# Second gather buffer, three 2 MB weight loads held until its rows have landed, and 30 fill transposes in the router of a decoder-layer kernel

## The reference

```python
m, new_a, new_b, v = token_mixer(x, ...)          # projections, convolutions, norms
h = layer_norm(ALPHA * x + m, ln1_g, ln1_b)
# moe_ffn(h): router, then experts
logits = h @ router_w + router_b
probs = softmax(logits)                            # best group of 4 by its top-2 sum, its top 2 experts, weights
for e in range(16):
    u = silu(h @ w_gate[e]) * (h @ w_up[e])        # 1024 x 512 each
    out = out + gates[:, e:e+1] * (u @ w_down[e])  # 512 x 1024
y = layer_norm(ALPHA * h + out, ln2_g, ln2_b)
```

## Time and profile before

| what | value |
|---|---|
| median of 3 runs | 1049.32 us |
| profiled execution, its own time | 1048.14 us |
| its span | 1046.4 us |
| TensorE busy | 995.1 us (95%), mean granted clock 0.978 |
| VectorE busy | 792.4 us (76%) |
| ScalarE busy | 473.1 us (45%) |
| GpSimd busy | 372.4 us (36%) |
| moved by DMA | 190.52 MB, 182 GB/s over the span |
| busy share of the DMA engines, in tenths, 40 slices | 7433232323232221333235534548899999999574 |
| granted TensorE clock, in tenths, 40 slices | 9999999999999999999999999997899999999995 |

### The profile page before, as it was taken

The page is one execution under the profiler, slowest core; times in us unless marked ns, Lnnn a source line. Parts: engine busy times, 40 slices in busy tenths (PEclk is TensorE's granted clock), DMA queues, the critical chain, the costliest instruction groups (busy, mean ns, idle before and its releaser), DMA issues.

```text
span 1046.4 us, 19478 instructions
## 1 busy us (share of the span) xinstructions
PE 995.1 (95%) x7212; PEld 901.5 (86%) x7212; DVE 792.4 (76%) x965; ACT 473.1 (45%) x665; POOL 372.4 (36%) x275
## 2 busy tenths in 40 slices
PE   7999999999999999999999999995999999999980
PEld 7999999999999998999999999974677777777760
DVE  2698889888999995744434598147789898999986
ACT  4232222323232244334442323424678787878763
POOL 2444434444544770445454544410110000000362
PEclk9999999999999999999999999997899999999995
DMA  7433232323232221333235534548899999999574
GB/s 220 122 93 95 85 100 81 100 80 100 81 101 81 80 82 49 100 110 89 81 99 170 172 90 144 208 163 317 300 368 391 375 391 379 383 388 393 203 253 165
DMA packets 163400, 190.52 MB, mean 182 GB/s; under 512 B 6675, under 2 KB 114195, under 8 KB 163340
## 3 DMA queue, kind: packets, MB, share of 16 engines
q1 hardware_dynamic: 156619, 177.65, 49.8%
q0 software_dynamic: 3008, 10.55, 3.2%
q10 hardware_dynamic: 3729, 1.75, 0.7%
HBM read 179.16 MB, written 11.76 MB: 182 GB/s over the span
## 4 chain that ended last, share of the span: by engine, by line
PE 57%; issue 25%; POOL 12%; DVE 3%; DMA 2%; ACT 1%; POOLq 0%; DVEq 0%
PE pr L986 27%; PE pr L1172 16%; POOL w_lo L562 12%; PE work L1172 8%; PE work L1148 1%; DMA hs<-h_rows,ids 1%; PE work L1069 1%; PE pr L1198 1%; DVE w_gate_lo L1625 1%; PE pr L1088 1%; PE work L1191 1%; DMA y_b<-y_rows,slot_b 1%; DVE y_a L1793 0%; PE work L1096 0%; DVE y_b L1789 0%
## 5 line engine op out<-in xcount | busy, mean ns | idle before, releaser
L562 POOL TENSOR_TENSOR w_lo<-raw,w_hi 128x512 fp32r<-128x512 f32 x208 | 298.0, 1453 | 334.5 <-ACT w_hi L680 334.5
L986 PE MATMUL pr<-x_hi,w_hi 128*128 128x260 f32 x1264 | 255.0, 283 | 0.2 <-POOL w_lo L562 0.2
L986 PE MATMUL pr<-x_hi,w_lo 128*128 128x260 f32 x1264 | 254.7, 283 | 0.0
L986 PE MATMUL pr<-x_lo,w_hi 128*128 128x260 f32 x1264 | 254.3, 283 | 0.0
L684 ACT ACTIVATE ev<-pr 128x520 f32<-128x520 f32 x96 | 58.1, 605 | 375.1 <-PE pr L986 375.1
L986 PEld LDWEIGHTS pr<-x_hi,w_hi 128*128 128x128 f32 x1264 | 195.0, 189 | 0.5 <-POOL w_lo L562 0.4
L986 PEld LDWEIGHTS pr<-x_hi,w_lo 128*128 128x128 f32 x1264 | 195.0, 188 | 0.0
L986 PEld LDWEIGHTS pr<-x_lo,w_hi 128*128 128x128 f32 x1264 | 194.4, 188 | 0.0
L1355 DVE SCALAR_TENSOR_TENSOR work<-b_pad,par,work 128x512 f32<-128x512 f32 x224 | 148.2, 743 | 0.0
L680 ACT ACTIVATE w_hi<-raw 128x512 fp32r<-128x512 f32 x208 | 118.9, 623 | 4.9 <-DMA raw<-in_w_in_dram 2.6
L599 POOL DMA_INDIRECT hs<-h_rows,ids x16 | 20.2, 1260 | 256.4 <-DVE ids L1619 246.6
(11 more groups left out here) (337 smaller groups left out, 1704.5 us busy)
## 6 DMA issues: line engine op xcount, KB each, us to landing
raw<-in_w_in_dram SPq DMA_DIRECT2D x80, 512.0 KB, 3.7
w_gate<-in_expert_w_gate_dram SPq DMA_DIRECT2D x16, 2048.0 KB, 14.9
w_up<-in_expert_w_up_dram SPq DMA_DIRECT2D x16, 2048.0 KB, 14.3
w_down<-in_expert_w_down_dram SPq DMA_DIRECT2D x16, 2048.0 KB, 13.6
y_rows<-y_out SPq DMA_DIRECT2D x15, 384.0 KB, 13.1
raw<-in_w_a_out_dram SPq DMA_DIRECT2D x8, 512.0 KB, 3.6
raw<-in_w_c_out_dram SPq DMA_DIRECT2D x8, 512.0 KB, 3.7
raw<-in_w_b_out_dram SPq DMA_DIRECT2D x8, 512.0 KB, 3.6
```

What stands on the lines that cost most here:

```text
L562: pool.tensor_tensor(w_lo[:, slot, k], raw[:, slot, k], w_hi[:, slot, k].bitcast(F32), ALU.subtract).then_inc(w_split, 1)
L986: mm = pe.matmul(pr[slot][:, h, 0:HALF], w[:, slot, k, :], x[:, k, h * HALF:(h + 1) * HALF], start=(k == 0 and w is w_hi and x is hi), sto ...
```

## The change

Four things are changed between about 692 and 735 us.

1. A second buffer `hs_second` takes the rows of expert 1, in memory that `y_out` uses later. GpSimd's gather for it waits for the row numbers alone, no longer for the transposes of expert 0's rows. The later gathers go into `hs` as before; their count is one less.
2. On SyncE the load of expert 2's gate matrix moves ahead of the five stores of `h`. Expert 2's up matrix and the down matrices of experts 1 and 2 (6 MB) are issued once `hs_second` has landed. Before, the up matrix had no wait of its own, and the two down matrices waited for the gather of expert 0.
3. TensorE gets 30 fill transposes ahead of its wait for the router's choices.
4. The fills ahead of and behind `turn` of expert 0 go from 20 and 12 to 18 and 8.

```diff
+        hs_second = place("hs_second", "b_pad", [C, D], plus=6 * NTB * E * 4)
...
             expert_load(first, 0, TURN[0], "down")
+            expert_load(first, 2, TURN[2], "gate")
             h_out()
-            expert_load(first, 2, TURN[2], "gate")
+            sp.wait_ge(second_in, 16)
             expert_load(first, 2, TURN[2], "up")
-            sp.wait_ge(first.gathered, 16)
             expert_load(first, 1, TURN[1], "down")
             expert_load(first, 2, TURN[2], "down")
...
+            def gather_second():
+                pool.wait_ge(first.ids_ready, 3)
+                pool.indirect_dma_start(out=hs_second[:], out_offset=None, in_=h_rows,
+                                        in_offset=bass.IndirectOffsetOnAxis(ap=ids[:, 1:2], axis=0)).then_inc(second_in, 16)
...
-                    if m == 0:
+                    if m == 0 and ps is first:
+                        gather_second()
+                    elif m == 0:
                         gather(ps, 1, t + 1)
...
+            for _ in range(30):
+                pe.transpose(pr[0][:, 1, 0:P], ident[:], ident[:])
             pe.wait_ge(mb_ready, 1)
...
-            def turn(ps, t):
-                pe.wait_ge(ps.gathered, t * 16 + 16)
+            def turn(ps, t, second=False, late=16):
+                source = hs
+                if second:
+                    source = hs_second
+                    pe.wait_ge(second_in, 16)
+                else:
+                    pe.wait_ge(ps.gathered, t * 16 + late)
...
-                    keep_busy(20)
+                    keep_busy(18)
                 turn(ps, n0)
                 if ps is first:
-                    keep_busy(12)
+                    keep_busy(8)
...
-                    turn(ps, t + 1)
+                    turn(ps, t + 1, second=ps is first and m == 0, late=0 if ps is first else 16)
```

More of the change, by code:

```diff
@@ L310, in build @@
         begun = sem("begun")
+        second_in = sem("second_in")
         more_posm = sem("more_posm")
@@ L1143, in find_ids @@
                 mm.then_inc(ps.ids_mm, 1)
-            def turn(ps, t):
-                pe.wait_ge(ps.gathered, t * 16 + 16)
+            def turn(ps, t, second=False, late=16):
[5 more added lines that the diff above has]
+                    pe.wait_ge(ps.gathered, t * 16 + late)
                 for k in range(KB):
-                    mm = pe.transpose(work[0][:, k // 4, k % 4 * C:(k % 4 + 1) * C], hs[:, k * P:(k + 1) * P], ident[0:C, 0:C])
+                    mm = pe.transpose(work[0][:, k // 4, k % 4 * C:(k % 4 + 1) * C], source[:, k * P:(k + 1) * P], ident[0:C, 0:C])
                 mm.then_inc(ps.turned, 1)
```

## The result

The changed kernel takes 1053.63 us (median of 9 runs, 1051.87 to 1056.19), the kernel before 1046.49 us in the runs beside it. The ratio is 1.0052, with a 95% interval of 1.0035 to 1.0069: about 5.4 us slower (3.7 to 7.2). The two medians lie 7.1 us apart, at the upper end of that interval. The forecast was 3.8 us.

A forecast was written before the change was run, and what follows sets the result against it. TensorE was taken to pace the loop at 17.9 us per expert, with DMA slack used up. Queue lateness of 4.5 us less 0.7 of slack gave +3.8 on the 1049.3 us median: 1053 us, own range 1050 to 1055, with rivals 1043 to 1057.

The forecast's parts named there:

- Second buffer and the order of issues: At expert 1's gather: the second buffer by itself gives nothing; issue again at about 723.5 us, released by the row numbers.
- Held loads, 6.0 us for TensorE: At expert 0: expert 1's rows land in 4.3 us instead of 8.2, so TensorE's up product ends 6.0 us earlier.
- S: In the DMA queue: how much later the whole stream runs through the held loads; taken as 4.5 us, ends 3.7 and 6.2.
- way (a): Queue lateness at expert 1's store, from the loop's rate of 18.46 us per expert: 3.7 us.
- way (b): Queue lateness from the later start and moved transfers, less 5.3 us of early DMA idle time: 6.2 us.
- My slack of 0.7 us: At expert 11's landing and expert 12's copy: slack left in the kernel before, 0.2 for the landing, 0.5 for find_ids.
- TensorE's 6.0 us cancel: At the copies into y_out: TensorE's gain ends in ScalarE's wait for store landings, leaving 3.8 us later net.
- How the waits look: In the loop: ScalarE waits 10 to 15 us over 12 times, marks about 0.5 us per expert, period 18.4 us.
- Gate load early and fills: Ahead of the loop: expert 2's early gate load, the 30 fills (about 3.5 us) and the 18 and 8 change nothing.
- The gain stays: Rival, chance 0.15: the DMA queue makes up the lost time, so TensorE's 6.0 us remain, 1043.3 us.
- Slower through a late gather: Rival, chance 0.08: expert 1's gather takes 8.2 us despite the empty queue; end 7.8 us later, 1057 us.
- A queue as in (b): Rival, chance 0.18: queue start-up as inefficient as before, lateness 6.2 us, end 5.5 us later, 1055 us.

The follow-up runs named there:

- e8: The kernel before with one more 2 MB transfer in SyncE's queue behind expert 2's down load, to unused rows; ratio 1.0002 to the kernel before.
- e9: The kernel before with two more 2 MB transfers in SyncE's queue behind expert 2's down load, to unused rows; ratio 1.0047 to the kernel before.
- e4: The changed kernel with the stores of experts 0 to 13 issued from ScalarE's queue behind the copy into y_out; ratio 1.0015 to the kernel before.
- e5: The changed kernel with the stores of experts 0 to 12 issued by GpSimd into its own queue; ratio 0.9927 to the kernel before.
- e6: The kernel before with the stores of experts 0 to 12 issued by GpSimd into its own queue; ratio 0.9994 to the kernel before.
- e1: The changed kernel with SyncE's load order and waits of the kernel before, second buffer and fills kept; ratio 0.9981 to the kernel before.
- e10: The kernel before with all the changed fills alone: 30 more, and 18 and 8 around the first turn; ratio 0.9983 to the kernel before.
- e3: The changed kernel with expert 2's up load ahead of the wait, so two loads held instead of three; ratio 0.9979 to the kernel before.
- e2: The kernel before with the load order alone changed: expert 2's gate load early, three loads held for expert 1's rows; ratio 1.0051 to the kernel before.
- e12: The kernel before with 18 and 8 fills around the first turn instead of 20 and 12, without the 30; ratio 1.0001 to the kernel before.
- e11: The kernel before with only the 30 fills ahead of the wait for the router's choices; ratio 0.9998 to the kernel before.

## Why the prediction was right

**Second buffer and the order of issues.** Right. The gather of expert 1 went out at 725.99 - 3.1 = 722.9, half a us before 723.46, and still behind the row numbers.

**Held loads, 6.0 us for TensorE.** Right: no wait, up product of 5.58 us, its end at 735.2 against the 735 forecast. The landing took 4.1 us (4.3 assumed). The estimate of 2.9 us by the Trainium skill (DMA: Bandwidth & Descriptors, Anatomy of one DMA) was too short with an almost idle queue too; the landings with little ahead of them lay between 4.1 and 5.2 us in all profiles.

**S, the lateness of the queue.** The mechanism was right, the size low: 5.7 us at the store of expert 1 (798.0 against 792.3) where I took 4.5, between way (a) with 3.7 and way (b) with 6.2. The step that was mis-sized is the choice between the two. I took the rate of nine later experts as the better guide. With the issue at 727.0, as measured, instead of 727.8, (a) would give 2.9 and (b) 5.4, so (b), which counts the idle time, is the better account. e8 and e9 bear it out: the first transfer more fits into the 5.3 us of idle time and costs nothing that shows (0.2 us, -1.3 to 1.7), the second costs 4.7 us more. S isn't one number either: the stores land 7.2 us later for expert 0 and 4.3 to 5.9 us later for experts 1 to 11.

**What it is worth at the end.** The profiles show 5.0 us at copy 12, the times 5.4 (3.7 to 7.2), the forecast's net was 3.8, with ends of 3.0 and 5.5 (5.2 where it gives the chances). My slack of 0.7 us was too large (the part for find_ids is 0.2 to 0.3, see e4). At copy 12 it doesn't come in: both kernels wait there for the store of expert 11, which lands 5.0 us later. That 5.7 - 0.7 gives 5.0 as well is a coincidence.

That the forecast of 1053 us lies within 1 us of the measured 1053.63 is partly luck. It stands on the median of three runs, 1049.32; the nine runs beside the changed kernel have 1046.49. A base that was high by 2.8 us made up for a net that was low by 1.6 by the ratio, 3.3 by the two medians.

That TensorE's 6.0 us cancel was the central claim. e9 shows it: with the queue late and no gain for TensorE the loop ends where that of the changed kernel does. e5 against e6 shows the other side: where no copy waits for a landing the gain arrives in full. But it holds for a queue that is late, and not for every gain. A TensorE that is ahead also frees the slots earlier, and the loads go out earlier. In e1 and e10, whose loads are in the old order, TensorE is some 3 us ahead at expert 0, the queue follows, and copy 12 is still 3 us ahead (974.03 and 974.16 against 977.03).

**How the waits look.** 25.4 us in 8 waits, from which one subtracts 8 x 1.8 of usual idle: 11 us, within the 10 to 15 named. But not 12 waits of equal kind: one of 7.9 at copy 1, then none for four copies, then seven. Find_ids waits for its marks 7 times, 5.6 us once and 0.3 on average in the others, not 0.5 in every expert. After the long wait, and the fall of the clock that follows it, TensorE is late and the queue is not, so that it takes until copy 6 for the queue to be behind again. In between the period is 17.9 us. From the landing of expert 0's store (782.9) to that of expert 11's (985.0) it is 18.4 us in the mean, the one forecast. It is no constant of the queue, though: 18.46 in the kernel before, 18.3 in e9 and 18.2 in e3, where nearly every copy waits. The store landings took 16.6 and 16.1 us, then 13.9 to 15.7, and 16.0 to 17.1 only from expert 5 on, not 16 to 17 throughout. The forecast had the clock only at expert 0; it didn't see that the first long wait in the loop would make it fall again.

**Gate load early and fills.** Right in sum (e2 and e10 to e12); the 30 fills took 3.49 us, 3.5 forecast. But "nothing" holds for the time only: in the profiles of e10 to e12 the clock did not fall, with or without the 30.

**The rivals.** "The gain stays" fell: DMA engines at a share of 1.02 to 1.06 from 736 us on made nothing up. It needed the stores on another queue. "Slower through a late gather" fell with the landing of 4.1 us. "A queue as in (b)", +5.5 us, came nearer to the measured 5.4 than my 3.8; the interval of 3.7 to 7.2 doesn't part the two.

## What to carry to other kernels

When a transfer is held back to free the queue for another one, what counts is the later start plus the work that is moved behind it, less the idle time that the queue has left before its first urgent transfer; with no idle time left, nearly all of it arrives (here 4.7 of an estimated 5.5 us). This account rests on one kernel with a nearly full queue. In a queue that is full, look for the urgent transfer that has the least room (here a store into which the next expert's copy runs, not the weights) and give that one another queue, before anything is gained upstream; check first what the issue costs the engine that takes it over. A gain that ends at the first wait for a late landing shows in the profile as an early engine and an unchanged end.

## What the runs showed of the hardware

- SyncE was held in the issue itself while several loads of 2 MB were outstanding: 2.4 us in a store, up to 8.4 in a load, where 0.4 is usual. In the changed kernel this put off the first store until 6.3 us after its data was ready.
- The issue of a store by ScalarE held its next operation for 0.6 us (e4). Its issue by GpSimd took 0.56 us and cost nothing, since GpSimd idled 8 us ahead of it (e5).
- From another queue a store of 384 KB landed after a median of 6.4 us while 2 MB loads filled the engines (share about 1.04, e5); in their queue it took 16 (changed kernel).
- TensorE's clock fell to its lower level (1.2 GHz) in the waits for expert 1's rows of 2.98, 3.02, 3.09 and 3.13 us (before, e6, e8, e9) and stayed at 2.4 GHz in those of 1.31, 1.62, 1.96 and 2.92 us (e1, e11, e10, e12). The up product behind them took 7.4 to 7.8 us in the one case, 5.6 in the other. In the changed kernel it fell in the 5.65 us wait for the marks (782 to 788 us) and was at 1.2 GHz from 788 to 792 us.
